# A hybrid decoder layer with a mixture of experts: the order of the last down projections, and the pieces in which the last weights are fetched

## What is computed

```python
for e in selected experts of a token (4 of 32):
    gu  = xb @ w_gate_up[e] + b_gate_up[e]            # 1024 -> 2048
    gate, up = min(gu[::2], 7), clip(gu[1::2], -7, 7)
    act = gate * sigmoid(1.702 * gate) * (up + 1)
    y   = act @ w_down[e] + b_down[e]                 # 1024 -> 1024
    out[token] += router_weight * y
x = x + out
return rms_norm(x, norm_final)
```

## Time and profile before

| what | us |
|---|---|
| median of the timed runs | 1194.03 |
| lowest and highest of them | 1193.01, 1194.77 |
| time of the profiled execution | 1195.38 |
| its span in the trace | 1193.5 |
| TensorE busy | 1136.9 |
| TensorE's weight loads busy (beside it) | 575.2 |
| VectorE busy | 309.6 |
| ScalarE busy | 128.8 |

### The profile page before, as it was taken

One profiled execution on the slowest core, in us unless ns is written; L12 is line 12 of the kernel. 1 busy time (PEld: TensorE's weight loads), 2 busy tenths in 40 slices (PEclk: granted clock), 3 DMA queues, 4 the chain that ended last, 5 costly groups with the idle time before them and its releaser, 6 DMA issues.

```text
span 1193.5 us, 13281 instructions
## 1 busy us (share of the span) xinstructions
PE 1136.9 (95%) x5663; PEld 575.2 (48%) x5663; DVE 309.6 (26%) x737; ACT 128.8 (11%) x218; POOL 15.1 (1%) x39
## 2 busy tenths in 40 slices
PE   9999999999999999998989899999999897989897
PEld 8888888955434334342424243434434242425232
DVE  3678731536302022020202020212202020202021
ACT  4641111001000000000000000000000000000012
POOL 1000200000000000000000000000000000000000
PEclk9999999999999999999999999999999999999999
DMA  9844843659999999999999999999999999999994
GB/s 259 282 148 130 288 133 117 269 223 385 422 427 437 425 435 424 434 425 435 424 434 425 435 424 430 433 427 434 425 434 424 435 424 435 424 437 423 435 417 202
DMA packets 56251, 443.99 MB, mean 372 GB/s; under 512 B 7604, under 2 KB 32416, under 8 KB 36992
## 3 DMA queue, kind: packets, MB, share of 16 engines
q1 hardware_dynamic: 50912, 438.33, 88.9%
q10 hardware_dynamic: 4448, 2.43, 0.9%
q0 software_dynamic: 832, 2.37, 0.6%
HBM read 441.66 MB, written 1.45 MB: 371 GB/s over the span
## 4 chain that ended last, share of the span: by engine, by line
PE 65%; DMA 31%; DVE 2%; ACTq 1%; ACT 1%; issue 0%; SPq 0%; DVEq 0%; POOL 0%; POOLq 0%
PE bank L965 26%; DMA ring<-in_w_gate_up 24%; PE bank L619 13%; PE bank L1032 8%; DMA ring<-in_w_down 7%; PE bank L933 4%; PE bank L1071 3%; PE bank L880 2%; PE bank L848 1%; PE bank L837 1%; PE bank L957 1%; DVE cvg L1685 1%; PE bank L635 1%; PE bank L1056 1%; PE bank L1046 1%; PE bank L650 1%
## 5 line engine op out<-in xcount | busy, mean ns | idle before, releaser
L965 PE MATMUL bank<-ring,cvg 128*64 128x512 f32 x2040 | 454.3, 602 | 29.6 <-DMA ring<-in_w_gate_up 29.3
L965 PEld LDWEIGHTS bank<-ring,cvg 128*64 128x64 f32 x2040 | 145.3, 139 | 318.8 <-issue 274.1
L1032 PE MATMUL bank<-ring,cvg 128*64 128x512 f32 x1024 | 224.5, 593 | 12.0 <-DMA ring<-in_w_down 12.0
L1695 DVE TENSOR_SCALAR cvm<-bank 128x512 f32<-128x512 f32 x33 | 22.8, 692 | 638.1 <-PE bank L965 638.1
L619 PE MATMUL bank<-ring 128*128 128x256 f32 x768 | 170.1, 380 | 0.7 <-DVE ring L1281 0.4
L619 PEld LDWEIGHTS bank<-ring 128*128 128x128 f32 x768 | 144.3, 190 | 21.0 <-issue 1.2
L1032 PEld LDWEIGHTS bank<-ring,cvg 128*64 128x64 f32 x1024 | 75.2, 137 | 158.1 <-issue 158.1
L2100 ACT ACTIVATE cvm<-cvm 128x512 f32<-128x512 f32 x33 | 20.8, 630 | 527.7 <-DVE cvm L1695 527.7
L933 PEld LDWEIGHTS bank<-ltm,hn 128*128 128x128 f32 x480 | 55.9, 192 | 7.5 <-issue 7.5
L1071 PE MATMUL bank<-vb,ltm 128*128 128x512 f32 x128 | 58.0, 594 | 0.0
L933 PE MATMUL bank<-ltm,hn 128*128 128x128 f32 x480 | 56.4, 275 | 0.0
(11 more groups left out here) (356 smaller groups left out, 552.6 us busy)
## 6 DMA issues: line engine op xcount, KB each, us to landing
ring<-in_w_gate_up SPq DMA_DIRECT2D x55, 4096.0 KB, 34.8
ring<-in_w_down SPq DMA_DIRECT2D x56, 2048.0 KB, 36.4
ring<-in_w_gate_up SPq DMA_DIRECT2D x15, 2048.0 KB, 11.9
ring<-in_w_in SPq DMA_DIRECT2D x24, 1024.0 KB, 6.7
ring<-in_w_down SPq DMA_DIRECT2D x16, 1024.0 KB, 33.0
ring<-in_w_gate_up SPq DMA_DIRECT2D x5, 1024.0 KB, 9.3
ring<-in_w_out SPq DMA_DIRECT2D x4, 1024.0 KB, 5.0
ring<-in_w_up_ml SPq DMA_DIRECT2D x2, 1024.0 KB, 5.1
```

The costliest lines, as they stand in the source:

```text
L965: mm = pe.matmul(B[4 + half][side * SLOTS:(side + 1) * SLOTS, :], rows, w[:, (k % 2) * PIECE + at:(k % 2) * PIECE + at + HALF], start=Fals ...
L1032: mm = pe.matmul(B[6 + half][e * SLOTS:(e + 1) * SLOTS, :], actT[:, e, at:at + SLOTS], by_block(double(of[e]), 4)[:, j, half * HALF:(half ...
L1695: dve.tensor_scalar(g2, both[:, :, :, 0], SWIGLU_LIMIT, None, ALU.min).then_inc(sem("glu_g_ready"), 1)
```

## The change

The list `doubles` ends in another order: side 0 of both items of the last pair, then both sides of `LONE`, then side 1 of the pair's two items. The first four of these are fetched whole (2 MB, one transfer each, by the loop that fetches all others), the last two, `QUARTERED`, in four quarters of 512 KB each, the two items' quarters alternating; TensorE waits at each part `j` for its quarter.

TensorE's order becomes: `down` side 0 of the pair; the two transposes; `down_lone` side 0 and side 1; `down` side 1 of the pair, with `scatter_lone` put between its part 0 and its part 1 (`add_lone`); and then the pair's scatter for both tiles at the end (`scatter_last`), which now closes the sums. It waits for `ysb` half by half. ScalarE copies `LONE`'s half result first and then the pair's result, the first half as soon as bank 6 is done (`last_half_done`), the second when the whole side is (`double_done`).

```diff
--- before.py
+++ after.py
@@ -112,10 +112,11 @@
             released.extend((GU, a, i) for i in range(KC // 2))
     doubles.extend((GU, LONE, i) for i in range(KC // 2))
     released.extend((GU, LONE, i) for i in range(KC // 2))
-    fetch_down(N_GROUPS - 1)
-    released.extend((DN, col, side) for side in range(2) for col in weights_of(N_GROUPS - 1))
-    doubles.extend((DN, LONE, side) for side in range(2))
-    released.extend((DN, LONE, side) for side in range(2))
+    downs_at_end = [(DN, col, 0) for col in weights_of(N_GROUPS - 1)]
+    downs_at_end += [(DN, LONE, side) for side in range(2)]
+    downs_at_end += [(DN, col, 1) for col in weights_of(N_GROUPS - 1)]
+    doubles.extend(downs_at_end)
+    released.extend(downs_at_end)
     release_of = {d: i for i, d in enumerate(released)}
     assert len(set(doubles)) == len(release_of) == 6 * E
 
@@ -305,7 +306,8 @@
 
             return ring[:, place_at[d], :]
 
-        HALVED = doubles[-6:]
+        QUARTERED = doubles[-2:]
+        QUARTER = PIECE // 2
         FIRST, AHEAD = doubles[0], doubles[DOUBLES]
         ahead = cvm[:, :, :].rearrange("p a s -> p (a s)")
         place_at, turn_at, turns = {}, {}, [0] * DOUBLES
@@ -337,19 +339,21 @@
                 return f"w_full{2 * place}", mixer_turns(2 * place)
             return f"ring_full{place}", 0
 
-        def second_full(d):
-
-            i = HALVED.index(d)
+        def quarter_full(d, j):
+
+            if j == 0:
+                return full(place_at[d])
+            i = 3 * QUARTERED.index(d) + j - 1
             if i < MIXER_PLACES:
                 return f"w_full{2 * i + 1}", mixer_turns(2 * i + 1)
             return f"second_full{i}", 0
 
-        def half_here(eng, d, half):
-
-            if half == 0:
+        def quarter_here(eng, d, j):
+
+            if j == 0:
                 here(eng, d)
             else:
-                name, before = second_full(d)
+                name, before = quarter_full(d, j)
                 eng.wait_ge(sem(name), 16 * (before + 1))
 
         def left_here(eng, place, n):
@@ -476,7 +480,7 @@
                     fetch_row(FIRST, 0, ahead, fixed(FIRST[1]), "first_full")
 
             expert = {col: fixed(col) for col in range(FIXED)}
-            for i in range(DOUBLES, len(doubles) - len(HALVED)):
+            for i in range(DOUBLES, len(doubles) - len(QUARTERED)):
                 col = doubles[i][1]
                 if col not in expert:
                     if len(expert) == FIXED:
@@ -497,16 +501,15 @@
                     sp.wait_ge(sem("double_done"), i - DOUBLES + 2)
                     fetch_two(i, expert[col])
 
-            def fetch_half(d, half):
-                at = slice(half * PIECE, (half + 1) * PIECE)
+            def fetch_quarter(d, j):
+                at = slice(j * QUARTER, (j + 1) * QUARTER)
                 src = dn_v[bass.ds(expert[d[1]], 1), :, d[2], at].rearrange("e p c -> p e c")
-                sp.dma_start(by_block(double(d)[:, at], 1), src).then_inc(sem((second_full(d) if half else full(place_at[d]))[0]), 16)
-
-            for pair in (HALVED[0:2], HALVED[2:4], HALVED[4:5], HALVED[5:6]):
-                sp.wait_ge(sem("double_done"), doubles.index(pair[-1]) - DOUBLES + 1)
-                for half in range(2):
-                    for d in pair:
-                        fetch_half(d, half)
+                sp.dma_start(by_block(double(d)[:, at], 1), src).then_inc(sem(quarter_full(d, j)[0]), 16)
+
+            sp.wait_ge(sem("double_done"), len(doubles) - DOUBLES)
+            for j in range(4):
+                for d in QUARTERED:
+                    fetch_quarter(d, j)
 
             left = left_count(sp)
             with sp.If(left > 0):
@@ -1013,7 +1016,7 @@
                     if n == N_GROUPS - 1 and e == 0 and i == 1:
                         gather_lone()
 
-            def down(n, sides=(0, 1)):
+            def down(n, sides=(0, 1), between=None):
 
                 if sides[0] == 0:
                     pe.wait_ge(sem("turned_copied"), n * 2 + 2)
@@ -1021,9 +1024,11 @@
                 for side in sides:
                     of = [(DN, weights_of(n)[min(e, len(weights_of(n)) - 1)], side) for e in range(2)]
                     for j in range(4):
+                        if between and j == 1:
+                            between()
                         for d in of:
-                            if d in HALVED:
-                                half_here(pe, d, j // 2)
+                            if d in QUARTERED:
+                                quarter_here(pe, d, j)
                             elif j == 0:
                                 here(pe, d)
                         at = j * P + side * SLOTS
@@ -1035,12 +1040,12 @@
                                                skip_group_check=True)
                                 if j == 3 and half == 1 and (e == 1 or of[0] != of[1]):
                                     mm.then_inc(sem("double_done"), 1)
-
-            def down_lone(side, w, wait=None):
+                                if of[e] == doubles[-1] and j == 3 and half == 0:
+                                    mm.then_inc(sem("last_half_done"), 1)
+
+            def down_lone(side, w):
 
                 for j in range(4):
-                    if wait and j % 2 == 0:
-                        wait(j // 2)
                     at = j * P + side * SLOTS
                     for half in range(2):
                         mm = pe.matmul(B[4 + half][half * SLOTS:(half + 1) * SLOTS, :], actT_left[:, at:at + SLOTS],
@@ -1062,14 +1067,24 @@
                     mm = pe.transpose(B[to][:, t * P:(t + 1) * P], weighted[:, t, :], ident[:, :])
                 mm.then_inc(sem("weighted_turned"), 1)
 
-            def scatter(n, tiles=range(T)):
+            def scatter(n):
 
                 pe.wait_ge(sem("y_copied"), n * 2 + 2)
                 pe.wait_ge(sem("scat_ready"), n + 1)
-                for t in tiles:
+                for t in range(T):
                     for half in range(2):
                         pe.matmul(B[2 * t + half], scat[:, t, :], ysb[:, half * HALF:(half + 1) * HALF],
                                   start=False, stop=False, skip_group_check=True)
+
+            def scatter_last(n):
+
+                for t in range(T):
+                    for half in range(2):
+                        if t == 0:
+                            pe.wait_ge(sem("y_copied"), n * 2 + half + 1)
+                        mm = pe.matmul(B[2 * t + half], scat[:, t, :], ysb[:, half * HALF:(half + 1) * HALF],
+                                       start=False, stop=True, skip_group_check=True)
+                    mm.then_inc(sem("sums_done"), 1)
 
             def seed_sums():
 
@@ -1171,7 +1186,6 @@
             down(last, (0,))
             turn_act(N_GROUPS, 0, 4)
             turn_weighted(N_GROUPS, 5)
-            down(last, (1,))
             pe.wait_ge(sem("turned_copied"), N_GROUPS * 2 + 1)
             pe.wait_ge(sem("scat_ready"), N_GROUPS + 1)
 
@@ -1185,12 +1199,16 @@
 
             for side in range(2):
                 d = (DN, LONE, side)
-                down_lone(side, double(d), lambda half: half_here(pe, d, half)).then_inc(sem("double_done"), 1)
-                scatter(last, (side,))
-
-            pe.wait_ge(sem("lone_copied"), 2)
-            for mm in scatter_lone():
-                mm.then_inc(sem("sums_done"), 1)
+                here(pe, d)
+                down_lone(side, double(d)).then_inc(sem("double_done"), 1)
+
+            def add_lone():
+                pe.wait_ge(sem("lone_copied"), 2)
+                for mm in scatter_lone():
+                    pass
+
+            down(last, (1,), add_lone)
+            scatter_last(last)
 
             left = left_count(pe)
             with pe.If(left > 0):
@@ -2124,9 +2142,14 @@
             se.activation(rstd[:, :], rstd[:, :], ACT.Sqrt).then_inc(sem("root_warm"), 1)
             se.wait_ge(sem("act_turned"), N_GROUPS * 2 + 1)
             se.activation(actT_left, B[4], ACT.Identity).then_inc(sem("turned_copied"), 1)
-            take_y(N_GROUPS - 1)
             done_with(se, (DN, LONE, 1))
             se.activation(y_lone[0:SLOTS, 0:HALF], B[4][0:SLOTS, :], ACT.Identity).then_inc(sem("lone_copied"), 1)
+            for half in range(2):
+                if half == 0:
+                    se.wait_ge(sem("last_half_done"), 1)
+                else:
+                    down_done(se, N_GROUPS - 1)
+                se.activation(ysb[:, half * HALF:(half + 1) * HALF], B[6 + half], ACT.Identity).then_inc(sem("y_copied"), 1)
 
             left = left_count(se)
             with se.If(left > 0):
```

## The result

| | before | after |
|---|---|---|
| median of the timed runs, us | 1194.85 (8 runs) | 1197.25 (8 runs) |
| lowest and highest | 1193.01, 1195.71 | 1196.29, 1197.81 |
| profiled execution, us | 1195.38 | 1197.19 |
| its span | 1193.5 | 1195.3 |

The changed kernel takes 1.0021 of the time before (95% interval 1.0013 to 1.0030), 2.4 us more: small, but clear of the spread. A second set of 11 runs of the same kernel gave 1197.27 against 1194.78, ratio 1.0018 (1.0009 to 1.0027).

A forecast was written before the change was run, and what follows sets the result against it. TensorE and transfers were both near full, the last landing deciding the end; after the change TensorE would. Profiled 1195.38 + 1.04 + 1.60 for the fallen clock = 1198.0, or 1196.7 against the median; range 1194.1 to 1198.2.

The forecast's parts named there:

- Step 1: First `down`: must wait for both whole side 0 transfers, starting at 1160.15 with a new stall of 2.7 us.
- step 5: The first `down`'s 32 records: clock falls behind the stall in three of five cases, costing 1.60 us.
- 2: TensorE's work in order from the first `down`: `down_lone` waits for ScalarE's copy, starts at 1168.62; part 3 starts at 1182.58.
- X: Start of part 3 of the pair's `down` side 1: 1182.58 with the clock held, 1184.18 with it fallen.
- Step 4: Behind the start of part 3: ScalarE's last copy, table load and `Sqrt` delay the first square to 1187.01, 1.04 us later.
- Step 3: End of the stream: last quarter lands at about 1181.0, wanted at 1182.58, so 1.6 us of cover; quarters cost nothing.
- the bound of the gain: Rival at the end, stream still decides: first square 0.49 us earlier, time 1193.5, the most to gain; chance 0.08.
- the sum with the clock held: Rival at the first `down`: stall without a fall of the clock, +1.04 us, 1195.1 against the median; chance 0.34.
- the rival of the dear quarters: Side 1 transfers: over 0.2 us per quarter uses up the cover; 2.5 us each gives 1213; chance 0.04.

The follow-up runs named there:

- the filler: Changed kernel plus five 256-column matmuls, result overwritten, in the stall ahead of the first `down`: 1195.51 us against 1194.78; with copies on VectorE too, 1195.75 against 1194.58.

## Why the prediction was right

The prediction had 1196.7, +2.7 us on the median of 1194.03; measured are +2.4 and +2.5. In absolute terms 1197.25 is 0.6 above it, because the median of the kernel before was 1194.85 over eight runs where the prediction had three. Held against the second profile of the changed kernel, which has the clock fallen, term by term:

| step | predicted, us | measured, us |
|---|---|---|
| 1: last `gate_up` piece to the first `down` | 9.81 | 9.88 |
| 1: stall ahead of it | 2.7 | 2.79 |
| 5: the 32 records, clock fallen | 8.69 | 8.78 |
| 2: first `down` to `down_lone` (with 1.60 of step 5) | 10.07 | 10.24 |
| 2: wait for ScalarE's copy | 0.6 | 0.56 |
| 2: first `down` to X (with 1.60 of step 5) | 24.03 | 24.32 |
| 4: X to the first square | 4.43 | 4.35 |

X is 3.43 us behind the start of the 24 records. Step 5 is borne out by the filler: the trace with it is shorter by 1.69 us, and by nothing else. Of the five profiled executions here with such a stall at the first `down` and no filler, the clock fell in four (8.44, 8.78, 8.58 and 8.78 us for the records) and held in one (7.09); the prediction had taken three of five. The twelve traces have many more stalls of 2.5 to 3.2 us ahead of 32 such records, earlier in the mixture: behind 33 of 54 the records took 8.44 us or more, behind the other 21 they took 7.09, and nothing lies between. That is three of five again. It also says how much the filler's two traces (7.09 in both) show by themselves: with two stalls in five harmless anyway, two harmless ones in a row would come by chance in about one case of six. What supports the filler beyond that is its median, 1.8 us below the changed kernel. Step 4's table load is shown by the copies on VectorE, worth 0.42 in the trace, where 0.6 had been the distance to the sums; VectorE's slower copies (0.69 us each in that trace, for 0.60) take part of the rest. Step 1 as the root of all is shown from both sides: without the whole transfers the loss is gone, and with them alone, in the kernel before, it is all there.

Step 3 came to the right end with a mis-sized term. The last quarter was taken to land where the last half did, 30.7 us behind `gate_up`'s piece. It landed 29.6 and 29.7 behind it, so the cover was 4.3 us in the changed kernel in place of the 3.2 that the sum has with the clock fallen. The last landing of the one trace before was late by about 1 us against its own pace, which the prediction could have seen: 1181.02 is 10.7 behind 1170.32 for 4 MB, where step 1 had put 9.9 on 4 MB. For the same reason the 0.49 us that it gave as the bound of the gain was too tight. Without the stall the trace gains 0.93 and the median 1.1.

One reading of the kernel before was wrong, though the sum doesn't hang on it. The prediction took the last landing for what decides the end, with TensorE waiting 0.71 us for it at 1181.02. That wait is in the row of the weight loads. The chain of the kernel before, and TensorE's own waits for `down` weights at the end (who, for whom: us in total, times, longest), name the landing ahead of 1170.32:

```profile
1131.06 39.12 DMA ring<-in_w_down
1170.32 3.65 PE bank L1032 x16
1179.32 3.64 PE bank L1046 x16
PE bank L1032 <- DMA ring<-in_w_down: 1.5, 2, 1.3
```

The waits are 1.5 us in two pieces, 0.15 and 1.31, and none at `down_lone` (L1046). Behind 1170.32 TensorE works through, and the late last half cost it 0.2 us: `down_lone` side 1 took 3.64 in the chain where side 0 took 3.43. So TensorE had about 1.7 us of slack behind the first `down` in the kernel before, and a stall of 2.8 us is more than that, even with the clock held.

The measured change of 2.4 lies between the sum with the clock held (+1.04) and that with it fallen (+2.64), nearer to the second, and on the bound of what can be told from no change. How many of the timed executions had the clock fallen can't be seen: each run has a granted clock on record, but as a mean over the whole span, and it doesn't separate them. If it is three in five, the mean change by the prediction's own terms is +2.0. That the median came as near as it did to the fallen case is in part luck. So is the side of the bound: the prediction put 0.60 on no difference that can be told and 0.37 on slower (its own parts add up to 0.39), and the two sets of runs have ratios of 1.0021 and 1.0018 around its bound of 0.2%.

## What to carry to other kernels

Where two transfers are both needed for the first matmul of a piece, fetch them in alternating parts: here the same bytes in the same stream, but whole, made the engine stand 2.8 us ahead of the first use, and behind it stood so much work that it was not made up. Finer parts at the very end of the stream pay only if the work ahead of them is in time. And a short wait costs more than its length where the engine behind it has no slack: here 2.8 us of standing still brought another 1.4 to 1.7 us at half clock.

## What was not expected of the hardware

The clock fell behind a stall of 2.12 us (in the kernel before with side 0 whole) and held behind one of 2.79 (with the copies on VectorE), so the length of the stall alone doesn't tell; one execution of the kernel before has it both ways. Over all twelve traces, 1.9 to 2.5 us of standing still were followed by slow records in 44 of 102 cases, 2.5 to 3.2 us in 33 of 54. With work in the stall whose result is thrown away (2.42 us of matmuls) the granted clock stayed at 1.00, in both traces that have it.

The last landing of the stream came 30.7 us behind that of the last `gate_up` weights in the one trace of the kernel before, and 29.4 to 30.0 behind it in the eleven others. This isn't the doing of the quarters, since kernels that end in 1 MB halves have it too: 29.4 (side 1 in halves, with the stall), 29.6 (without it) and 29.8 (the kernel before with side 0 whole). What made the last half of that one trace late isn't shown.

In a full queue, transfers of half the size cost no measurable time each. In the changed kernel the eight quarters landed 1.2 to 1.3 us apart, the last 10.0 us behind the landing ahead of the first; in the kernel with side 1 in halves and no stall, the four 1 MB halves of the same side landed 2.5 us apart, the last 9.8 behind. With this the rival of the dear quarters is out.
